# Queries rotated before their 1/rms, which goes into the scale of the softmax exponential, and their squares summed by turned blocks on VectorE

## The reference

```
q = axial_rope(rmsnorm(aq.reshape(B, S, ATTN_HEADS, ATTN_HEAD_DIM), q_norm_w), tabs)
k = axial_rope(rmsnorm(ak.reshape(B, S, ATTN_KV_HEADS, ATTN_HEAD_DIM), k_norm_w), tabs)
...
qc = rmsnorm(aqc.reshape(B, L, ATTN_HEADS, ATTN_HEAD_DIM), q_norm_w)
...
s = jnp.einsum('blhgd,bmhd->bhglm', qg, kc).astype(jnp.float32) * ATTN_HEAD_DIM ** -0.5
p = jax.nn.softmax(jnp.concatenate([s, s_sink], axis=-1), axis=-1)
```

## Time and profile before

| | |
|---|---|
| median of three runs | 2241.78 us |
| span of the profiled execution | 2241.7 us |
| granted TensorE clock | 1.00 in each of the stretches read below |
| TensorE busy | 2213.3 us (99%) |
| VectorE busy | 1390.7 us (62%) |
| ScalarE busy | 901.4 us (40%) |
| DMA | 300.84 MB, 134 GB/s |

### The profile page before, as it was taken

The page is one execution under the profiler, slowest core; times in us unless marked ns, Lnnn a source line. Parts: engine busy times, 40 slices in busy tenths (PEclk is TensorE's granted clock), DMA queues, the critical chain, the costliest instruction groups (busy, mean ns, idle before and its releaser), DMA issues.

```text
span 2241.7 us, 29868 instructions
## 1 busy us (share of the span) xinstructions
PE 2213.3 (99%) x12353; PEld 1926.7 (86%) x12353; DVE 1390.7 (62%) x1907; ACT 901.4 (40%) x1340; POOL 194.5 (9%) x264
## 2 busy tenths in 40 slices
PE   7999999999999999999999999999999999999999
PEld 6888888978888888898888898888889899999997
DVE  5998822668567565587763267665236967667754
ACT  3322222556644454342222143222126666555442
POOL 0000000000333340000000000000000033330000
PEclk9999999999999999999999999999999999999999
DMA  8876622211221312346552236565323233336864
GB/s 290 238 220 185 197 94 94 86 48 41 94 76 57 94 57 89 115 135 190 159 177 94 94 113 194 182 188 169 111 97 96 60 113 114 113 118 194 242 180 160
DMA packets 302431, 300.84 MB, mean 134 GB/s; under 512 B 9648, under 2 KB 269336, under 8 KB 302296
## 3 DMA queue, kind: packets, MB, share of 16 engines
q1 hardware_dynamic: 301872, 298.76, 43.1%
q10 hardware_dynamic: 424, 0.18, 0.0%
HBM read 297.86 MB, written 1.05 MB: 133 GB/s over the span
## 4 chain that ended last, share of the span: by engine, by line
PE 87%; DVE 6%; ACT 2%; DMA 2%; POOL 2%; issue 1%; SPq 0%; ACTq 0%; DVEq 0%
PE PS L1784 13%; PE PS L1790 13%; PE PS L1785 13%; PE PS L1770 6%; PE PS L1771 6%; PE PS L1772 6%; PE PS L1804 4%; PE PS L1809 4%; PE PS L1805 4%; PE PS L2340 2%; DMA raw<-in_ffn_w 1%; DVE WL L1091 1%; PE PS L2399 1%; PE PS L2351 1%; PE PS L2076 1%
## 5 line engine op out<-in xcount | busy, mean ns | idle before, releaser
L1091 DVE TENSOR_TENSOR WL<-raw,WH 128x1024 fp32r<-128x1024 f32 x416 | 502.3, 1245 | 345.0 <-ACT WH L666 344.2
L666 ACT CAST WH<-raw 128x1024 fp32r<-128x1024 f32 x416 | 416.4, 1047 | 378.4 <-PE PS L1772 259.5
L1784 PE MATMUL PS<-hH,WH 128*128 128x512 f32 (+1 forms) x1536 | 541.8, 363 | 1.3 <-DVE sg L1341 0.8
L1785 PE MATMUL PS<-hL,WH 128*128 128x512 f32 (+1 forms) x1536 | 538.2, 361 | 0.0
L1790 PE MATMUL PS<-hH,WL 128*128 128x512 f32 (+1 forms) x1536 | 335.4, 361 | 0.0
L1784 PEld LDWEIGHTS PS<-hH,WH 128*128 128x128 f32 x1536 | 290.1, 189 | 46.2 <-issue 1.2
L1785 PEld LDWEIGHTS PS<-hL,WH 128*128 128x128 f32 x1536 | 290.1, 189 | 44.2 <-issue 1.2
L1790 PEld LDWEIGHTS PS<-hH,WL 128*128 128x128 f32 x1536 | 263.9, 189 | 44.2
L1117 DVE SCALAR_TENSOR_TENSOR mraw<-mraw,cst 128x1024 f32<-128x1024 f32 x196 | 242.5, 1281 | 21.5 <-DMA mraw<-in_w_mod 18.5
L1770 PE MATMUL PS<-hidH,WH 128*128 128x512 f32 (+1 forms) x576 | 214.4, 372 | 0.0
L1771 PE MATMUL PS<-hidL,WH 128*128 128x512 f32 (+1 forms) x576 | 213.9, 371 | 0.0
(11 more groups left out here) (265 smaller groups left out, 3509.6 us busy)
## 6 DMA issues: line engine op xcount, KB each, us to landing
raw<-in_ffn_w SPq DMA_DIRECT2D x176, 512.0 KB, 5.2
mraw<-in_w_mod SPq DMA_DIRECT2D x132, 512.0 KB, 4.7
raw<-in_w_in SPq DMA_DIRECT2D x52, 1024.0 KB, 5.3
raw<-in_ffn_w SPq DMA_DIRECT2D x44, 1024.0 KB, 4.9
raw<-in_w_branch_attn SPq DMA_DIRECT2D x8, 1024.0 KB, 5.1
raw<-in_w_branch_gla SPq DMA_DIRECT2D x8, 1024.0 KB, 5.1
raw<-in_w_out SPq DMA_DIRECT2D x8, 1024.0 KB, 5.1
mfirst_b<-in_w_mod SPq DMA_DIRECT2D x8, 512.0 KB, 10.8
```

Source lines behind the costliest of these rows:

```text
L666: nc.scalar.copy(half(WH, n % 2, e, rows), half(raw, n % 2, e, rows)).then_inc(hi_ready, 1)
L1091: nc.vector.tensor_tensor(half(WL, n % 2, e, rows), half(raw, n % 2, e, rows), half(WH, n % 2, e, rows).bitcast(F32), ALU.subtract).then_i ...
L1784: mm(o, wh[:, kt, cols], rh[:, kt, 0:T], start=kt == 0, stop=False)
L1785: mm(o, wh[:, kt, cols], rl[:, kt, 0:T], start=False, stop=False)
```

## The change

- ScalarE copies a query tile times the weight out of PSUM (`weighted`), without 1/rms, into one of two buffers in turn (`rotated_buf`: `qn` for odd j, `qrs` for even). This is rotated and split as before.
- ScalarE's squares of the two tiles stand side by side. VectorE adds them in turned blocks of 32x32: one reduction with transposition per j gives 32 numbers per partition in layer 0 and 16 in layer 1 (`square_sums`). TensorE folds four heads at a time (`q_sums`) by four matmuls, each with 32 columns of the folding matrix and a quarter of the output's partitions. The result has the queries on the partitions.
- ScalarE takes exp(-0.5 ln(sum + 128 eps)) of it (`q_rsq`). This is 1/rms times 128^-0.5, and is the scale operand of the exponential, one number per partition, where the constant stood. In `maxima` one instruction for a negative scaled maximum and a minimum becomes two, with a wait.
- The keys are normalized as before. The order of all three engines in `attn_proj` is new.

```diff
@@ ScalarE
 def squares(j):
     act.wait_ge(half_done, 2 * (n + j + 1))
+    if j == 2:
+        act.wait_ge(qk_ss, 2 * (l + 1))
+    elif j > 2:
+        act.wait_ge(q_red, 4 * l + j - 2)
...
+def weighted(j):
+    act.wait_ge(half_done, 2 * (n + j + 1))
+    if j == 2:
+        act.wait_ge(qk_n, 2 * (l + 1))
+    else:
+        act.wait_ge(qk_ready, tile0 * l + 2 * (j - 2))
+    for e, (t, T) in enumerate(qk_tiles(l, j)):
+        nc.scalar.activation(rotated_buf(j)[:, e, 0:T], PS[:, 2 * (j % 3) + e, 0:T], ACT.Copy,
+                             scale=vecT[:, Q_NORM + l:Q_NORM + l + 1]).then_inc(q_n, 1)
+def q_rsq(g):
+    own = slice(g * GRP * qtokens(l) // P, (g + 1) * GRP * qtokens(l) // P)
+    act.wait_ge(q_tot, 2 * l + g + 1)
+    nc.scalar.activation(rq[:, own], PS[:, 6, own], ACT.Ln, bias=epsc[:, 2:3]).then_inc(q_ln, 1)
+    act.wait_ge(q_ln, 2 * l + g + 1)
+    nc.scalar.activation(rq[:, own], rq[:, own], ACT.Exp, scale=-0.5).then_inc(q_rs, 1)
...
+prep(n + 2)
+squares(1)
+prep(n + 3)
+squares(2)
+k_rsq()
+weighted(2)
+prep(n + 4)
+split(1)
+for j in range(3, 6):
+    if j > 3:
+        prep(n + j + 1)
+    if j == 5:
+        q_rsq(0)
+    weighted(j)
     squares(j)
-    if j > 1:
-        rsq(j - 1)
-    if j > 2:
-        split(j - 2)
+    split(j - 1)
 prep(n + 7)
 gate_copy(l, 0, 0)
-rsq(5)
-split(4)
+split(5)
 exps(l, 0)
 gate_copy(l, 1, 7)
-split(5)
+q_rsq(1)
 gate_copy(l, 2, 6)
@@ exps
-                     scale=SCALE, accum_out=small[:, 16 + g:17 + g])
+                     scale=head_scales(l)[:, GRP * kv + g, qb:qb + 1], accum_out=small[:, 16 + g:17 + g])
@@ VectorE
+def square_sums(j):
+    dve.wait_ge(q_sq, 8 * l + 2 * (j - 1))
+    own = slice((j - 2) * qtokens(l) // 16, (j - 1) * qtokens(l) // 16)
+    nc.vector.tensor_reduce(qred[:, own], squares_buf(l, j).rearrange("p (b i) -> p b i", i=32), AX.X, ALU.add,
+                            apply_transpose=True).then_inc(q_red, 1)
...
+prep(n + 2)
+prep(n + 3)
+k_normed()
+cosines(1)
+square_sums(2)
+prep(n + 4)
+sines(1)
+rotated(1)
+cosines(2)
+low(1)
+for j in range(3, 6):
+    if j > 3:
+        prep(n + j + 1)
+    sines(j - 1)
+    rotated(j - 1)
+    cosines(j)
+    square_sums(j)
+    low(j - 1)
 prep(n + 7, only=0)
-low(4)
-normed(5)
+sines(5)
+rotated(5)
 maxima(l, 0)
-cosines(5)
-sines(5)
+low(5)
 scale(l, 0)
-rotated(5)
-low(5)
 prep(n + 7, only=1)
@@ maxima
+    dve.wait_ge(q_rs, 2 * l + kv + 1)
...
-    nc.vector.scalar_tensor_tensor(small[:, 8 + 2 * e:10 + 2 * e], small[:, two], -SCALE, ns, ALU.mult, ALU.min)...
+    by = head_scales(l)[:, GRP * kv + 2 * e:GRP * kv + 2 * e + 2, qb]
+    nc.vector.scalar_tensor_tensor(small[:, 8 + 2 * e:10 + 2 * e], small[:, two], -1.0, by, ALU.mult, ALU.mult)...
+    dve.wait_ge(at_scaled, done + 1)
+    nc.vector.tensor_tensor(small[:, 8 + 2 * e:10 + 2 * e], small[:, 8 + 2 * e:10 + 2 * e], ns, ALU.min)...
@@ TensorE
+def q_sums(g):
+    pe.wait_ge(q_red, 4 * l + 2 * (g + 1))
+    pe.wait_ge(qk_ln, 2 * (l + 1))
+    w = GRP * qtokens(l) // P
+    parts = qred[:, 4 * g * w:4 * (g + 1) * w].rearrange("p (x u) -> p u x", u=4)
+    for u in range(4):
+        lanes = slice(32 * u, 32 * u + 32)
+        ins = mm(PS[lanes, 6, g * w:(g + 1) * w], fold[:, lanes], parts[:, u], start=True, stop=True)
+    ins.then_inc(q_tot, 1)
...
+pe.wait_ge(v_ready, 2 * l + 2)
+unit_cols(n + 2, 4, hH, hL, qtokens(l))
+k_sums()
+unit_cols(n + 3, 0, hH, hL, qtokens(l), between=3 * [nothing] + [lambda: swaps(1)] + 3 * [nothing])
+swaps(2)
+pe.wait_ge(qk_parts, tile0 * l + 2)
+unit_cols(n + 4, 2, hH, hL, qtokens(l))
+swaps(3)
+q_sums(0)
+pe.wait_ge(qk_parts, tile0 * l + 4)
+unit_cols(n + 5, 4, hH, hL, qtokens(l))
+swaps(4)
 pe.wait_ge(qk_parts, tile0 * l + 6)
 gate_cols(l, 0, 0)
-swaps(4)
-qk_sums(5)
+swaps(5)
 scores(l, 0)
-pe.wait_ge(qk_ln, tile0 * (l + 1))
-gate_cols(l, 1, 7, 0, KT // 2)
-swaps(5)
-gate_cols(l, 1, 7, KT // 2, KT)
+q_sums(1)
+gate_cols(l, 1, 7)
+pe.wait_ge(q_ln, 2 * (l + 1))
 gate_cols(l, 2, 6)
```

More of the change, by code:

```diff
@@ L144, in hybrid_backbone @@
         rstd = sb("rstd", [P, T2])
+        qred = sb("qred", [P, HEADS * T2 // 32])
+        rq = sb("rq", [P, HEADS * NTB])
         with ExitStack() as r:
@@ L789, in rsq @@
-                def rsq(j):
-                    for e, (t, T) in enumerate(qk_tiles(l, j)):
[L791 to L797, removed]
+                        nc.scalar.activation(squares_buf(l, j)[:, e * T:(e + 1) * T], PS[:, 2 * (j % 3) + e, 0:T],
+                                             ACT.Square).then_inc(qk_sq if j == 1 else q_sq, 1)
@@ L1375, in attn_proj, with k_normed @@
                                             ALU.subtract).then_inc(v_ready, 1)
[L1377 to L1383, removed]
+                def k_normed():
+                    for e in range(2):
+                        dve.wait_ge(qk_rs, 2 * l + e + 1)
+                        nc.vector.scalar_tensor_tensor(qn[:, e, :], PS[:, 2 + e, :], vecT[:, K_NORM + l:K_NORM + l + 1], qrs[:, e, :],
                                                        ALU.mult, ALU.mult).then_inc(qk_n, 1)
@@ L1407, in low @@
                         lo = kL[:, e, 0:T] if j == 1 else actL[:, 2 * (j - 2) + e, 0:T]
[L1408 to L1421, removed]
+                        nc.vector.tensor_tensor(lo, rotated_buf(j)[:, e, 0:T], hi.bitcast(F32), ALU.subtract).then_inc(qk_ready, 1)
+                prep(n + 2)
[16 more added lines that the diff above has]
+                    low(j - 1)
                 prep(n + 7, only=0)
-                low(4)
-                normed(5)
+                sines(5)
+                rotated(5)
                 maxima(l, 0)
-                cosines(5)
-                sines(5)
+                low(5)
                 scale(l, 0)
-                rotated(5)
-                low(5)
                 prep(n + 7, only=1)
@@ L2167, in attn_proj, with k_sums @@
                 first_two(3 * l + 1, rows_high, rows_low, 2, 1)
[L2169 to L2173, removed]
-                        mm(PS[:, 6 + e, 0:T], ones[:], qsq[:, e, 0:T], start=True, stop=True).then_inc(qk_ss, 1)
+                def k_sums():
+                    for e in range(2):
+                        pe.wait_ge(qk_sq, 2 * l + e + 1)
+                        mm(PS[:, 6 + e, :], ones[:], qsq[:, e, :], start=True, stop=True).then_inc(qk_ss, 1)
@@ L2176, in swaps @@
                 def swaps(j):
                     for e, (t, T) in enumerate(qk_tiles(l, j)):
-                        pe.wait_ge(qk_n, t + 1)
-                        mm(PS[:, 2 * (j % 3) + e, 0:S], swap[:], qn[:, e, 0:S], start=True, stop=True).then_inc(qk_swap, 1)
-                for j in range(2, 6):
-                    if j == 2:
-                        pe.wait_ge(v_ready, 2 * l + 2)
-                    elif j > 3:
-                        pe.wait_ge(qk_parts, tile0 * l + 2 * (j - 3))
-                    unit_cols(n + j, 2 * (j % 3), hH, hL, qtokens(l))
-                    if j > 2:
-                        swaps(j - 2)
-                    qk_sums(j - 1)
+                        if j == 1:
+                            pe.wait_ge(qk_n, 2 * l + e + 1)
+                        else:
+                            pe.wait_ge(q_sq, 8 * l + 2 * (j - 2) + e + 1)
+                            pe.wait_ge(q_n, 8 * l + 2 * (j - 2) + e + 1)
@@ new lines, in swaps @@
+                        mm(PS[:, 2 * (j % 3) + e, 0:S], swap[:], rotated_buf(j)[:, e, 0:S], start=True, stop=True).then_inc(qk_swap, 1)
+                pe.wait_ge(v_ready, 2 * l + 2)
[5 more added lines that the diff above has]
+                unit_cols(n + 4, 2, hH, hL, qtokens(l))
```

42 lines of the change are left out of this document (31 added, 11 removed).

## The result

The changed kernel takes 2251.99 us (median of four runs, 2249.16 to 2253.29); the kernel before 2241.83 beside it. The ratio is 1.0042, with a 95% interval of 1.0030 to 1.0054: slower by 10.2 us, where 5.2 us less was forecast. It lies outside the range.

The account below looks back on a forecast made before the run. The prediction took TensorE to bound the kernel. Layer 0 5.3 us shorter, layer 1 1.5 shorter and the sets 1.6 longer gave 5.2 us off 2241.7: 2236.5 us, range 2233.8 to 2240.3.

Parts of the forecast that it names:

- stretch of layer 0: Layer 0, from the keys' sums to the first turned probabilities: 59.9 us instead of 65.2, 5.3 us shorter.
- stretch of layer 1: Layer 1, from the keys' sums to the first turned probabilities: 39.8 us instead of 41.3, 1.5 us shorter.
- sets, added: Attention sets: the maxima's extra instruction makes four waits for probabilities 0.4 us longer each, 1.6 us in all.
- the sums' matmuls: TensorE's ones-matmuls for the queries: four pairs go in each layer, worth 6.9 us in layer 0, 3.8 in layer 1.
- the folds: TensorE's new quarter-width matmuls in `q_sums`, twice a layer: 0.5 us a call, 1.0 us in each layer.
- the second rival: Quarter-width folds on TensorE go one after the other: 2.2 us a call instead of 0.5, total 2241.6; 5%.
- the row of quarter-width passes: Earlier trace on TensorE: sixteen quarter-width passes busy 1.07 us, so their weight loads of 0.110 us cannot each be waited for.
- the keys' norm: Layer 1: both squares wait for both key sums, the norm begins later, and TensorE's key swaps wait 0.85 us.
- the new wait: Layer 1, gate tile 2: TensorE waits for the logarithm in `q_rsq(1)`, 2.1 us.
- the scale operand costs ScalarE time: Rival: fetching the exponential's per-partition scale costs 0.19 us each, 6.1 us on top, total 2242.6; 6%.
- VectorE as the bound of layer 1: Rival: VectorE falls behind by some 0.5 us in each of three units, total 2238.5 to 2240; 21%.
- The waits that fall into one another: Rival: early layer 1 waits absorb later ones and the sets' 1.6 falls to 0.4; 2233.8 to 2234.5 us; 10%.

Follow-up runs that it names:

- moved: The changed kernel with its two new buffers at the end of the attention's memory, so older buffers keep their old addresses: 2238.09 us, ratio 0.9983.
- after128: The changed kernel with an unused buffer of 128 bytes a partition behind rq, making the shift 768 bytes: 2237.33 us, ratio 0.9982.
- early: As moved, with ScalarE's second logarithm and exponential of the query sums placed before the first set's exponentials: 2234.49 us, ratio 0.9966.
- onemax: As cscale, without the extra instruction of the maxima, as before the change; queries' 1/rms left out of the scores: 2233.67 us, ratio 0.9965.
- cscale: As moved, with the exponential's scale constant again and the maxima's extra instruction kept; queries' 1/rms left out of the scores: 2236.50 us, ratio 0.9979.

## Why the prediction was wrong

**The step that failed** is the sentence under the sum: "Nothing behind the attention changes: loads start when a weight's buffer is free, and shift with it." It looked at the order of the work and at the loads, and not at the two lines of the diff that allocate `qred` and `rq`. That nothing ahead of the attention changes, the prediction took for granted without a word. On both sides of it the 640 bytes cost 13.9 us (2251.99 less 2238.09), shown in two ways: put into the kernel before they cost 13.4 us, and with the old addresses, or with 128 bytes more, the changed kernel runs at 2238.09 or 2237.33 us, inside the forecast's range. No rival came near it: slower had 4 in 100, from mishaps in the attention alone.

**The attention went nearly as the steps say.** By one profile of each, without the shift (`moved`):

| step | forecast | measured |
|---|---|---|
| stretch of layer 0 | 59.9 | 60.16 (60.13 in the changed kernel) |
| stretch of layer 1 | 39.8 | 40.00 (41.42 in the changed kernel) |
| sets, added | 1.6 | 1.24 + 0.73 = 1.97 |
| sum | -5.2 | -4.4 |

The stretches take 5.0 and 1.3 us off, and the sets give 2.0 back. The medians say 3.9. The range held these kernels; the forecast of 2236.5 is 0.8 under `after128`.

That it came so near is in part luck, since two terms of the sum were too large and cancel. The stretches of `moved`:

```profile
436.86:497.02 60.16, 59.31 (x269) 47.30 (x268) 38.42 (x72) 29.59 (x54) 0.00 (x0) 1.00 0.23 69
1711.40:1751.40 40.00, 36.63 (x270) 32.65 (x269) 33.42 (x72) 24.00 (x54) 0.00 (x0) 1.00 0.35 106
```

TensorE's busy time fell by 5.9 us in layer 0 (65.20 to 59.31) and by 2.5 in layer 1 (39.09 to 36.63). With the two calls of folds, 0.27 us each as read below, what went is 6.4 and 3.0 us, where the sum has 7.2 (6.9 and 0.3) and 3.8. So the sums' matmuls were priced 0.8 us too high in each layer, and the folds 0.5 too high in each.

In the sets, too, the sum of 1.97 is near the 1.6 forecast, but the listed waits did not each grow by 0.4. In `moved` the two short ones did (0.52 to 0.93 and 0.36 to 0.73), the two long ones stayed at 1.3, and one of 0.2 was new. Ahead of layer 0's long one a wait of 0.21 for `ptL` had come, and its set was 0.4 us later all the same.

**The folds.** TensorE's timeline of the changed kernel, about the second call in layer 1:

```profile
1755.29 0.39 PE L1832 MATMUL PS<-kL,actH 128*128 128x512 f32 x1
1755.52 0.39 PE L1833 MATMUL PS<-kH,actL 128*128 128x512 f32 x1
1755.84 0.25 PE L2242 MATMUL PS<-qred,fold 128*32 128x8 f32 x8
1756.02 0.39 PE L1865 MATMUL PS<-hH,WH 128*128 128x256 f32 x1
```

From 1755.52 to 1756.02 is 0.50, and 0.23 of it is the matmul ahead: a call costs 0.27 us, not 0.5, and the second rival's 2.2 is out. With weight loads of 0.108 us each, eight in a row would take 0.86 by themselves, so these loads overlap although all of the folds read the same rows. The rule that the prediction quoted from the Trainium skill (TensorE: Matmul & The Clock Gate, The mechanism) does not hold for these quarter-width weights, and the row of quarter-width passes that spoke against it was right. The same section also lets a load go ahead when it targets the background weight buffer, which the prediction left out. The full-width loads of this kernel overlap as well: in layer 0's stretch they are busy 50.19 of 65.20 us, and TensorE has no gap. The turned reduction of 512 took 0.70 us, as read.

**The waits** are within 0.2 us of the forecast but for the keys' norm, 0.4 for 0.85. Layer 1 still loses 1.4 us in the changed kernel against `moved`, and this is the granted clock. The timeline of the changed kernel, then that of `moved`, at the matmul that waits for the logarithm:

```profile
1761.35 0.58 PE L1865 MATMUL PS<-hH,WH 128*128 128x256 f32 x1 [2.19 <-ACT rq L835]
1761.73 0.41 PE L1866 MATMUL PS<-hL,WH 128*128 128x256 f32 x1
1761.94 0.41 PE L1865 MATMUL PS<-hH,WH 128*128 128x256 f32 x1
```

```profile
1748.42 0.39 PE L1865 MATMUL PS<-hH,WH 128*128 128x256 f32 x1 [2.20 <-ACT rq L835]
1748.64 0.28 PE L1866 MATMUL PS<-hL,WH 128*128 128x256 f32 x1
1748.76 0.28 PE L1865 MATMUL PS<-hH,WH 128*128 128x256 f32 x1
```

The wait is the same, 2.2 us. Behind it the matmuls start 0.21 us apart in one execution and 0.12 in the other, and the granted clock from 1760 to 1764 is 0.65, part of it at the lower level of 1.2 GHz. In the profile of `after128` the clock falls at the same place, in that of `moved` it doesn't. So the new wait, priced at its own length, has a further price that comes and goes. In `moved` the four runs with a mean clock of 0.999 took 2238.8 to 2240.3 us and the six at 1.000 2237.2 to 2238.3; in `early`, which has no such wait, all six are at 1.000. In `after128` the price is hardly seen: four runs at 0.999 took 2237.5 to 2238.0 us, six at 1.000 2236.4 to 2237.9. That the fall comes of the wait is argued from its place and from `early`, not shown.

**The rivals.** The first (the scale operand costs ScalarE time) is true in kind, 0.09 us an exponential, half of the 0.18 from which it was to decide, and worth 0.5 us in the sets. The folds one after the other: no. VectorE as the bound of layer 1: no, since the waits for its work there are 0.4 and 0.5 us and the stretch came out at 40.00. The waits that fall into one another: only between `onemax` and `cscale`, where layer 1's stretch, too, is 0.5 us shorter (39.32 for 39.80), and the wait for the logarithm went from 2.04 to 1.63: two instructions fewer stand ahead of the first set's exponentials, behind which the logarithm stands.

## What to carry to other kernels

Read the allocations in a diff as you read its instructions: here a buffer of 640 bytes moved the operands of TensorE and cost over three times what the change brought. When the instructions are the same but later after every stage, compare the number of starts in a window of an untouched stage and try the new buffers elsewhere, or an unused one in the kernel before; keep moving operands and weights a multiple of 256 bytes apart in a partition when the matmuls have 512 columns, as far as these runs go (those of 256 columns gained about 1 ns where the others lost 6). And a wait for a tiny result (here a logarithm of 8 or 16 numbers a partition) should be looked for in the queue of the engine that makes it: `q_rsq(1)` placed ahead of the four exponentials of a set and a gate tile's copy was worth 3.6 us, nearly as much as the change.

## What the runs showed of the hardware

- The distance of fp32 matmuls of 512 columns that follow each other without a gap depends on where one operand's buffer stands to the other's: with a shift of 128, 384 or 640 bytes against the layout of before it is 233 ns instead of 227 on `hidH` and `hidL`, with 768 or 1280 bytes, or with both shifted by 640, it is as before. It is the same with the roles exchanged (`WH` streamed, `hidH` as weights: 232 to 233 for 226 to 227), and for `hH` and `hL` with the weights shifted by 128 (5.3 to 6.0 ns longer). Matmuls of 256 columns get about 1 ns shorter by the same shifts (119.8 to 118.6). 64 bytes cost 5.6 us of the 13.4.
- Why is open. The runs show a distance between buffers, modulo 256 bytes. They don't tell whether the read of the moving operand meets the loading of the next weights or something else, nor do they part `WH` and `WL` from `raw`.
- Eight weight loads of 32 columns, with passes of 8 streamed columns each, go through in 0.27 us.
- A scale per partition makes ScalarE's exponential with accumulation 0.09 us longer than a constant one, at 256 as at 512 elements (554 for 464 ns, 770 for 680).
- Behind the same idle time of 2.2 us the granted clock fell in the profiles of the changed kernel and of `after128` (0.65 from 1760 to 1764 us in the first) and stayed at 1.00 in that of `moved`.
